# Hidden steps in two halves: one projection group cut 4 + 4 instead of 5 + 2 + 1, and the spatial gate moved around step 5

## What is computed

```python
def compress(rows, params):                 # run on k_cmp and v_cmp, prompt and 8 sample batches
    w1, b1, w2, b2 = params
    blocks = ...                            # overlapping windows of 32 rows, stride 16
    return jax.nn.gelu(blocks @ w1 + b1) @ w2 + b2

def mixer_out(x, o_cmp, o_sel, o_win, gl, za, u, v, zb, r, lw):
    ...
    v_n = layernorm(jax.nn.gelu(v), lw['v_norm_g'], lw['v_norm_b'])
    sgu = jax.nn.gelu(u) * spatial_gate(v_n, lw['w_spatial'], lw['b_spatial'])
    pb = (sgu * jax.nn.silu(zb)) @ lw['w_pb']
    ...
```

## Time and profile before

| | us |
|---|---|
| median of 3 runs | 622.34 |
| lowest, highest | 620.72, 622.7 |
| the profiled execution | 622.7 |
| its span, first to last instruction | 621.0 |

### The profile page before, as it was taken

One profiled execution on the slowest core, in us unless ns is written; L12 is line 12 of the kernel. 1 busy time (PEld: TensorE's weight loads), 2 busy tenths in 40 slices (PEclk: granted clock), 3 DMA queues, 4 the chain that ended last, 5 costly groups with the idle time before them and its releaser, 6 DMA issues.

```text
span 621.0 us, 12850 instructions
## 1 busy us (share of the span) xinstructions
PE 585.7 (94%) x5262; PEld 519.9 (84%) x5262; DVE 344.1 (55%) x846; ACT 248.2 (40%) x557; POOL 77.1 (12%) x129
## 2 busy tenths in 40 slices
PE   7899999999899999988999999999999999997993
PEld 5899999999788997977888887666577899997992
DVE  5632213787687653353373756767655457762265
ACT  5543345447133434332331544435453352231333
POOL 0025431121011124504200000000000000000000
PEclk9999999999889999989999999999999999998998
DMA  9347723351353244924521220201111423306103
GB/s 309 136 139 231 237 69 135 137 193 62 103 170 135 72 136 137 334 73 148 225 84 55 68 69 2 69 1 35 35 34 35 143 70 103 102 2 237 35 2 144
DMA packets 45709, 70.02 MB, mean 113 GB/s; under 512 B 4178, under 2 KB 36114, under 8 KB 45395
## 3 DMA queue, kind: packets, MB, share of 16 engines
q1 hardware_dynamic: 38016, 44.85, 22.7%
q0 software_dynamic: 6912, 23.24, 11.0%
q10 hardware_dynamic: 722, 1.12, 0.5%
HBM read 65.23 MB, written 8.13 MB: 118 GB/s over the span
## 4 chain that ended last, share of the span: by engine, by line
PE 66%; DVE 8%; issue 2%; ACT 2%; DMA 1%; SPq 0%; ACTq 0%; DVEq 0%
PE m L1629 39%; PE s L1936 4%; PE o L1950 4%; PE t L1943 3%; PE s L1811 2%; PE s L1812 2%; PE s L1814 2%; PE t L1775 2%; PE t L1838 1%; DVE w_lo L1214 1%; PE o L1897 1%; DMA U<-in_x_p 1%; PE s L1790 1%; DVE xt_sb L1369 1%; PE s L1852 1%
## 5 line engine op out<-in xcount | busy, mean ns | idle before, releaser
L1629 PE MATMUL m<-h_hi,w_hi 128*128 128x272 f32 x448 | 134.6, 300 | 0.5 <-DVE w_lo L1214 0.5
L1629 PE MATMUL m<-h_hi,w_lo 128*128 128x272 f32 x448 | 129.8, 290 | 0.0
L1629 PE MATMUL m<-h_lo,w_hi 128*128 128x272 f32 x448 | 129.5, 289 | 0.0
L1629 PE MATMUL m<-w_hi,h_hi 128*128 128x256 f32 (+2 forms) x360 | 105.5, 293 | 4.2 <-DVE U L1577 2.0
L1629 PE MATMUL m<-w_hi,h_lo 128*128 128x256 f32 (+2 forms) x360 | 102.9, 286 | 0.0
L1629 PE MATMUL m<-w_lo,h_hi 128*128 128x256 f32 (+2 forms) x360 | 102.9, 286 | 0.0
L1629 PEld LDWEIGHTS m<-h_hi,w_hi 128*128 128x128 f32 x448 | 84.9, 190 | 10.6 <-issue 8.0
L1214 DVE TENSOR_TENSOR w_lo<-raw,w_hi 128x1024 fp32r<-128x1024 f32 (+2 forms) x62 | 71.1, 1154 | 35.3 <-ACT w_hi L951 35.2
L1629 PEld LDWEIGHTS m<-h_lo,w_hi 128*128 128x128 f32 x448 | 85.2, 190 | 0.0
L1629 PEld LDWEIGHTS m<-h_hi,w_lo 128*128 128x128 f32 x448 | 85.1, 190 | 0.0
L1629 PEld LDWEIGHTS m<-w_hi,h_hi 128*128 128x128 f32 (+1 forms) x360 | 68.8, 191 | 5.9 <-DVE U L1577 2.3
(11 more groups left out here) (294 smaller groups left out, 968.1 us busy)
## 6 DMA issues: line engine op xcount, KB each, us to landing
raw<-in_w_in SPq DMA_DIRECT2D x36, 512.0 KB, 3.6
U<-in_x_p SPq DMA_DIRECT2D x8, 512.0 KB, 7.0
raw<-in_w_o SPq DMA_DIRECT2D x8, 512.0 KB, 3.9
raw<-in_w_in SPq DMA_DIRECT2D x8, 256.0 KB, 3.3
U<-in_ck_win POOLq DMA_DIRECT2D x8, 256.0 KB, 3.4
U<-in_cv_win POOLq DMA_DIRECT2D x8, 256.0 KB, 6.2
raw<-in_w_pa SPq DMA_DIRECT2D x8, 256.0 KB, 4.1
raw<-in_w_pb SPq DMA_DIRECT2D x4, 512.0 KB, 3.3
```

What stands on the lines that cost most here:

```text
L1629: ins = mm(out, lhs(a, k), rhs(b, k), start=(k == 0 and a + b == 0), stop=(k == n - 1 and a == 1))
```

## The change

Four things change in `plan()` and in what reads the list.

- The group of a pair step is cut in two halves of four k tiles: the first half before `xt` 2, the second before `xt` 3, so that no part stands between `xt` 3 and `kc`, and the whole group (its `main` entry too) comes before `xt` 3. `take()`, `("part", ...)` and `PARTED` are gone.
- The `main` entry is where ScalarE evacuates the group, and it now stands before `xt` 3 on ScalarE also. The `mix` entries are gone: VectorE multiplies at the `main` entry.
- `ln` 4 and `lnr` stand after `hidh` 2 instead of after `hidh` 3. `ln2` 0 to 2 stand after `hidh` 3, `ln2` 3 and 4 after `hidh` 4.
- All five `sp` stand around step 5: 0 and 1 ahead of `xt` 5, 2 ahead of `hid` 5, 3 and 4 behind it. Before, they stood at steps 5 (0 and 1), 6 (2 and 3) and 7 (4).

```diff
     for c in range(1, NCH):
         behind = [("hidl", c - 1)] if c - 1 in PAIRS else []
         if c == 5:
-            order += [("xt", 5, 0)] + behind + [("sp", 0), ("w1hi", 1), ("hid", 5), ("kc", 4), ("w1lo", 1), ("sp", 1)]
+            order += [("xt", 5, 0)] + behind + [("sp", 2), ("w1hi", 1), ("hid", 5), ("sp", 3), ("kc", 4), ("w1lo", 1), ("sp", 4)]
             main(1)
-            order += [("ln2", 2), ("ln2", 3)]
             continue
         order += [("xt", c, 0), ("xt", c, 1)] + behind
         if c == 1:
             main(1)
-        if c == 8:
-            order.append(u1[0])
-        s, after = take()
-        order += [("part", s, 0, 5), ("xt", c, 2), ("part", s, 5, 7), ("xt", c, 3), ("part", s, 7, 8), ("kc", c - 1), ("hidh", c)]
-        order += ([s] if c != 7 else []) + [x for x in after if x not in (("ln", NT), ("lnr",))] + extra.get(c, [])
+        order += [("half",) + groups[state["n"]][1:], ("xt", c, 2)]
+        main(1)
+        n = order.index(groups[state["n"] - 1]) + 1
+        after = order[n:]
+        del order[n:]
+        order += [("xt", c, 3), ("kc", c - 1), ("hidh", c)] + after
+        order += {3: [("ln2", i) for i in range(3)], 4: [("ln2", 3), ("ln2", 4), ("sp", 0), ("sp", 1)]}.get(c, [])
     order += [("hidl", NCH - 1)]
-    main(1)
-    order += [("mix", u1[3]), ("kc", NCH - 1)]
+    main(AFTER_LAST_HIDDEN)
+    order += [("kc", NCH - 1)]
...
-                elif kind == "mix":
...
+                elif kind == "main" and SLOTS[s[1]][0][0] in "UZ":
...
+                    if name[0] == "U":
+                        wait_main_read(dve, s)
+                        x = sg[:, 2 * int(name[1]) + a, c]
+                        if k == 0:
+                            wait_evacuated(dve, T_AT[("sp", NT)])
+                        v.tensor_tensor(x, x, f, ALU.mult).then_inc(mix_fn, 1)
...
-                        wait_evacuated(dve, T_AT[("sp", 0)])
+                        wait_evacuated(dve, T_AT[("sp", 3)])
...
+                    ks = range(KD // 2) if kind == "half" else range(KD // 2, KD) if s in HALVED else range(KD)
```

More of the change, by code:

```diff
@@ L245, in plan @@
     order += [("qT", i) for i in range(NT)] + [("qTs",)]
-    def take():
-        n = len(order)
-        main(1)
[L251 to L258, removed]
     order += [("w1hi", 0), ("xt", 0, 0)]
@@ L368 @@
 MAIN_AT = {s: n for n, s in enumerate(MAIN)}
+HALVED = [("main",) + s[1:] for s in ORDER if s[0] == "half"]
 def freed_by(s):
@@ L449, in slot_used @@
     return max(n for n, x in enumerate(MAIN) if x[1] == sl) + 1
-PARTED = [s[1] for s in ORDER if s[0] == "part"]
 DIRECT = [("main", SLOT["U0"], 0, hf) for hf in range(2)]
@@ L1306, in _ @@
                     v.tensor_tensor(sg[:, 0, tok(i)], sg[:, 0, tok(i)], sp_t[:, 0:r], ALU.mult).then_inc(t_dve, 1)
-                elif kind == "mix":
[L1308 to L1315, removed]
+                elif s in DIRECT:
+                    continue
+                elif kind == "main" and SLOTS[s[1]][0][0] in "UZ":
                     name, n, k = SLOTS[s[1]][0], MAIN_AT[s], FN_AT[s]
@@ L1688, in _ @@
                     ins.then_inc(t_done, 1)
-                elif kind == "main" and s in PARTED:
-                    continue
-                elif kind in ("main", "part"):
-                    ks = range(KD)
-                    if kind == "part":
-                        _, s, k0, k1 = s
-                        ks = range(k0, k1)
-                    n = MAIN_AT[s]
-                    if ks[0] == 0:
+                elif kind in ("main", "half"):
+                    n = MAIN_AT[("main",) + s[1:]]
+                    if s not in HALVED:
                         wait_main_bank(pe, n)
@@ L1719, in _ @@
                         continue
-                    if n and ks[0] == 0:
+                    if n and s not in HALVED:
                         pe.wait_ge(lo_done, 2 * sl + 2)
                     hx, wx = (h_hi, h_lo), (w_hi, w_lo)
+                    ks = range(KD // 2) if kind == "half" else range(KD // 2, KD) if s in HALVED else range(KD)
                     if mk in ("tm", "wo"):
@@ L1746, in _ @@
                         ins = passes(out[:, 0:HALF], lhs, lambda b, k: hx[b][:, k, hf * HALF:(hf + 1) * HALF], KD, ks=ks)
-                    if ks[-1] < KD - 1:
+                    if kind == "half":
                         continue
```

27 lines of the change are left out of this document (14 added, 13 removed).

## The result

| | before | changed |
|---|---|---|
| median, us | 620.82 (20 runs, 619.45 to 625.48) | 625.08 (20 runs, 622.05 to 626.79) |
| profiled execution, us | 622.7 | 627.23 |
| its span, mean granted clock | 621.0, 0.983 | 625.5, 0.985 |

The ratio, which is taken over all runs and not from the two medians, is 1.0054, 95% interval 1.0037 to 1.0073: slower by 0.54%, about 3.4 us (the medians differ by 4.3). Measured again beside further runs of the kernel before, it was 1.0041 (1.0017 to 1.0064), 2.5 us (the medians differ by 2.9). The forecast was +5.7. The sign was right and the time lies in the range of 623.0 to 632.0, but the size was too large: by the ratios, measured were 0.45 to 0.6 of it.

What follows compares the result with a forecast made beforehand. TensorE was taken to bound the kernel, with 66% of the chain that ended last. Step terms summed to +4.0 us at full clock, plus +1.7 for the clock: +5.7, a median of 628.0 us, range 623.0 to 632.0.

Steps and rivals of the forecast that it cites:

- Halves for parts: In each hidden step, cutting the group in two halves makes TensorE wait for VectorE: +0.60 us a step.
- Floor 1: Before xt 2: it needs the bank VectorE empties by two subtractions, so comes no sooner than 1.72 us after hidl.
- floor 2: Before hidh: it needs VectorE's copy, so comes no sooner than 1.70 us after xt 3.
- Product ahead of the copy: Steps 6 to 9: VectorE multiplies by the gate before its copy, delaying the copy and hidh: +0.43 us a step.
- `ln` 4 and the root: Step after hidh 2: a third statistics group delays ScalarE's root and the casts and table load queued behind: +2.5 us.
- Three `ln2`: Step after hidh 3: root refinement and three ln2 on VectorE delay xt 2, leaving TensorE 2.3 us idle: +2.68 us.
- Steps 7 to 9: Last three hidden steps, 12.48 us each with sp 2 to 4 and ln2 4 gone: -2.02, -0.56 and +1.03 us.
- all of `sp` around `hid` 5: From hidh 4 to hidh 6: old low clock and waits exchanged for new waits and the floors, 29.99 for 30.25: -0.26 us.
- the clock: Hidden steps: after new idle stretches TensorE's clock falls once and returns after a short stretch: +1.7 us.
- Rival B: Clock falls before hid 5 and stays low through it: +9.1 us, 631.4 us; chance 0.12.
- A: Rival: the idle stretches are there but the clock does not fall: +4.0 us, 626.3 us; chance 0.23.
- C: Rival: queueing half absorbed, late root not binding, floor 2 0.12 lower, some 0.5 saved elsewhere: +1.2, 623.5 us; chance 0.13.

Runs made afterwards that it cites:

- after_filled: The changed kernel with matmuls that nobody reads added in its three idle stretches; 622.18 us, ratio 1.0008 to the kernel before.
- cut_only: The kernel before with only its groups cut 4 + 4, gelu and gate product staying behind hidh; 624.37 us, ratio 1.0041.
- cut_gate: The kernel before with the 4 + 4 cut and the gate work's new places, but gelu and product still behind hidh; 623.04 us, ratio 1.003.
- gate_only: The kernel before, parts and products unmoved, with only ln 4, the root, the ln2 and the sp in their new places; 620.21 us, ratio 0.998.
- after_again: The changed kernel once more, unchanged, beside further runs of the kernel before; 624.91 us, ratio 1.0041.
- gate_ln4_early: As gate_only, with the statistics of ln 4 moved ahead to before hid 0 and the root left after hidh 2; 617.35 us, ratio 0.9936.
- after_root_back: The changed kernel with ln 4 and the square root back behind hidh 3, the three ln2 still behind them; 626.35 us, ratio 1.0066.
- under_hid: The kernel before with ln 4's statistics before hid 0, root and ln2 0 behind hidh 3, ln2 1 to 3 under hid 5; 612.18 us, ratio 0.985.

## Why the prediction was right and where it was wrong

**What held.** The bound, the floors, the queueing and the sign. Predicted at full clock were intervals of 12.06, 14.0, 14.12, 29.99 and three of 12.48; with the idle stretches filled (after_filled) they read 11.89, 13.80, 14.01, 29.22, 12.47, 12.46, 12.46. By steps:

- *Halves for parts*, +0.60: +0.46 to +0.55 (cut_only). Floor 1 was right (1.71 for 1.72 us), floor 2 is 0.06 lower than reckoned (1.64 for 1.70), half of what the lower bound allowed.
- *Product ahead of the copy*, +0.43: +0.48 (cut_gate against the changed kernel). The copy started 1.17 us after `xt` 3, as predicted; the timeline of steps 7 to 9 in TensorE (`xt` 3) and VectorE reads

```profile
203.67 0.60 PE L1761 MATMUL t<-cst,U 128*128 128x128 f32 x4
...
204.37 0.44 DVE L1309 TENSOR_TENSOR sg<-sg,tmp 128x272 f32<-128x272 f32 x1 [1.33 <-PE t L1761]
204.84 0.69 DVE L1353 CAST xt_sb<-t 64x512 fp32r<-64x512 f32 x1
```

- *`ln` 4 and the root*, +2.5: +2.3 (13.79 less 11.5, the cut included; +1.9 without it, in gate_only). The root started 7.25 us after `hidh` 2 (7.35 was predicted), and ScalarE's casts released `hidh` 3. ScalarE's timeline, against the earlier trace rows:

```profile
141.02 0.21 ACT L1035 ACTIVATE st<-st 128x5 f32<-128x5 f32 x1 [6.38 <-DVE st L1263]
141.13 2.35 ACT L1056 CAST xt_sb<-t 64x512 fp32r<-64x512 f32 x4
```

- *Three `ln2`*, +2.68: +2.57 with the clock filled. *Steps 7 to 9*: to 0.03 us.
- The waits before `xt` 2 of steps 3 and 4 and before `xt` 5 were to be 2.0, 2.3 and 2.9; they are 1.76, 2.04 and 2.77.

**Where the size went wrong.** The forecast of +5.7 was +4.0 at full clock and +1.7 for the clock; measured were +3.4 (and +2.5). The mechanisms were right; what failed is the size of two terms of the sum, "all of `sp` around `hid` 5" and "the clock".

*"All of `sp` around `hid` 5" was forecast at -0.26 and came to -1.03* (29.22 us in after_filled for 30.25; the other two profiled executions of the kernel before had 29.36 and 31.50, so the sure part is 29.22 for the 29.99 of the working). TensorE's timeline in after_filled, whose `hidh` 4 began at 160.17, reads (`xt` 5, `xt` 6, `xt` 2 of step 6)

```profile
168.90 0.71 PE L1767 MATMUL t<-cst,U 64*128 64x64 f32 x8 [0.41 <-DVE sg L1296]
...
181.69 1.26 PE L1763 MATMUL t<-cst,U 128*128 128x128 f32 x8
...
185.27 0.66 PE L1763 MATMUL t<-cst,U 128*128 128x128 f32 x4 [0.81 <-DVE xt_sb L1360]
```

After `hidh` 4 these are 8.73, 21.52 and 25.10 us, where the working had 8.9, 22.04 and 25.85. No single wait makes the 0.8: `sp` 2 took 0.89 for the estimated 1.05, `hid` 5 was through at 15.78 for 16.15, and the wait before `xt` 2 was 0.81 and not 1.3. The floors and the queueing of steps 2 to 4 were 0.1 to 0.2 too high each. Together the sum at full clock was 1.3 too high: after_filled takes 106.3 us from `hidh` 1 to `hidh` 9, the kernel before 103.65, so +2.7 and not +4.0.

*"The clock" was one new fall, +1.7, with the kernel's other falls left standing.* In each of three profiled executions of the changed kernel there are two new ones in the hidden steps; over after_filled's 106.31 they cost 2.6, 4.6 and 2.9 us (108.88, 110.89 and 109.17), 3.3 on average. The fall at 275 us stood in two of three profiled executions of the kernel before and in none of three of the changed one; its going, worth 1.7, is likely the change's doing, but no run isolates it. The fall at 19 us came in one of three and in two of three.

So in the profiled executions alone the forecast would have looked right: three of each give 109.6 and 103.8 us for the stage on average (the kernel before: 103.65, 102.81, 104.96), +5.8, and 627.2 and 621.1 us for the whole, +6.1. There the two errors cancel, which is luck. All three of the changed kernel, at clocks of 0.984 or 0.985, took 627.1 to 627.4, some 2.3 above the median; the four best of its 21 runs, at 0.993, took 622.05 to 623.0. Those of the kernel before, 622.7, 619.26 and 621.39, stand on both sides of its median. So a forecast made against one profiled execution was a forecast of profiled executions.

The mean clocks say the same. Span times one less the mean clock, as a measure of the time lost, is on average 10.1 us in the kernel before (35 runs) and 7.6 in the changed one (21 runs); in the profiled ones it is 9.7 and 9.6. Two to three us of it in every run belong to the low clock behind the last matmul, which costs nothing. The timed runs of the changed kernel thus lost some 2 us less than its profiled ones, about one fall fewer (an estimate: a fall of 3.4 us counts 1.7), and that is the difference between +6.1 and the measured +3.4 to +4.3. Which fall they lack is not recorded.

**The base** was a smaller error: the median of three runs, 622.34, is 620.8 to 622.05 with 19 to 35 runs.

**The rule on transposes.** All three idle stretches ended in transposes. In three profiled executions of the changed kernel the stretches behind them lasted 3.4 us five times and 6.8 us once, never the 10 of the kernel before, and the wait of 1.76 to 1.78 us before `xt` 2 of step 3 brought none. The Trainium skill (TensorE: Matmul & The Clock Gate, Part 4: PE-mode transpose) says that transposes do not count as busy time in the way matmuls do; longer stretches would have followed from it, and the trace does not show them. That does not refute the rule, since the transposes lasted only 0.4 to 0.6 us before matmuls followed (158.34 after 157.93, 171.85 after 171.21). And the stretch of 10.2 us in the kernel before lay behind a wait that ended in the matmuls of `hid` 5, not in transposes. Rival B (a low clock through `hid` 5) did not come about: the median of `hid` 5's matmuls is 275 ns in all three executions, though in after_again the low stretch reached its first ones (421 ns at most).

**Rivals A and C.** The measured times, 624.9 and 625.1, lie between A (626.3) and C (623.5), some 1.3 us from each, but neither mechanism was seen: the clock did fall, and ScalarE's root did bind (gate_ln4_early, after_root_back). Of C's three parts one did not hold (the root), floor 2 is lower by half of what it assumed, and some 0.8 us was indeed saved elsewhere, in the interval 4-6.

**What stays open.** Why the timed executions of the changed kernel keep a higher mean clock than all three profiled ones: of a timed run only the mean is recorded. Nor do the runs show why the low clock before `hid` 5 lasted 10.2 us in two executions and 6.8 in another, with the same instructions in them, nor what brought the fall at 275 us, before which TensorE's longest wait was 0.9 us.

## What to carry to other kernels

Where the bounding engine has just enough work to cover another engine's latency, moving three matmuls of 0.125 us out from under it costs time at every step: 0.46 to 0.55 us a step here. The cut alone (ratio 1.0041) cost about as much as the whole change (1.0054 and 1.0041). Work of a helper engine belongs behind the copies that the bounding engine waits for, and beside a long phase that needs nothing else from it: under_hid moved the gate's work by that rule and gained 1.5%. A clock that falls after idle stretches is costed as falls before against falls after, over several profiled executions, because one execution of the kernel before differed from another by 3.4 us.
